# One decoder step on one core: the groups of sample value matmuls stand behind other projection units

## The reference

```python
def attn_sample(...):
    past_ckv = cache_ckv_l[page_table].reshape(db, -1, KV_LORA)
    past_kr = cache_kr_l[page_table].reshape(db, -1, ROPE_DIM)
    ...
    s_past = jnp.einsum('bthk,bsk->bhts', q_abs, past_ckv) + jnp.einsum('bthr,bsr->bhts', q_rope, past_kr)
    ...
    p = jax.nn.softmax(sc, axis=-1).astype(ckv.dtype)
    o_lat = (jnp.einsum('bhts,bsk->bthk', p[..., :n_past], past_ckv)
             + jnp.einsum('bhts,bsk->bthk', p[..., n_past:], ckv))
    ...
def combine(x, gate, att, g_att, pool, g_pool, w_out):
    mixed = jnp.concatenate([att * jax.nn.silu(g_att), pool * jax.nn.silu(g_pool)], axis=-1)
    return x + gate[:, None, :] * jnp.einsum('bte,ed->btd', mixed, w_out)
```

## Time and profile before

| | us |
|---|---|
| median of 3 runs | 1618.17 |
| lowest and highest run | 1617.62, 1657.11 |
| span of the profiled execution | 1616.8 |
| PE busy in it | 1483.7 (92%) |
| DVE busy | 780.6 (48%) |
| ACT busy | 651.9 (40%) |
| POOL busy | 493.5 (31%) |

### The profile page before, as it was taken

One profiled execution on the slowest core, in us unless ns is written; L12 is line 12 of the kernel. 1 busy time (PEld: TensorE's weight loads), 2 busy tenths in 40 slices (PEclk: granted clock), 3 DMA queues, 4 the chain that ended last, 5 costly groups with the idle time before them and its releaser, 6 DMA issues. The chain is left out here.

```text
span 1616.8 us, 24423 instructions
## 1 busy us (share of the span) xinstructions
PE 1483.7 (92%) x8584; PEld 1236.4 (76%) x8584; DVE 780.6 (48%) x1594; ACT 651.9 (40%) x1296; POOL 493.5 (31%) x423
## 2 busy tenths in 40 slices
PE   7787799999999589999999999999848999999997
PEld 1487689999998467777777787877627888888886
DVE  0587532223321677766676767664252333333333
ACT  0255322222110556565666666666631222222221
POOL 0355523232221524343443434343331111111100
PEclk9899899999999799999999999999957999999999
DMA  9243221111101200000000000000065144434310
GB/s 367 94 126 110 84 87 53 53 53 52 58 27 47 52 1 11 11 8 12 8 12 8 14 4 14 7 7 11 15 244 181 60 157 156 155 122 146 124 60 28
DMA packets 71502, 114.70 MB, mean 71 GB/s; under 512 B 33236, under 2 KB 50548, under 8 KB 69205
## 3 DMA queue, kind: packets, MB, share of 16 engines
q1 hardware_dynamic: 58782, 70.73, 13.8%
q0 software_dynamic: 3456, 27.26, 4.6%
q10 hardware_dynamic: 9168, 15.50, 2.7%
HBM read 90.95 MB, written 22.77 MB: 70 GB/s over the span
## 5 line engine op out<-in xcount | busy, mean ns | idle before, releaser
L1177 POOL TENSOR_TENSOR pt_lo<-pt,pt_hi 128x512 fp32r<-128x512 f32 (+2 forms) x160 | 171.1, 1069 | 262.3 <-ACT pt_hi L1082 261.9
L1081 ACT ACTIVATE pt<-att_ps_s 128x512 f32<-128x512 f32 (+1 forms) x320 | 170.2, 532 | 150.9 <-PE att_ps_s L1351 85.3
L1237 DVE TENSOR_REDUCE mx<-att_ps_p 128x1 f32<-128x512 f32 (+2 forms) x300 | 177.2, 606 | 91.7 <-PE att_ps_p L1321 71.4
L1082 ACT ACTIVATE pt_hi<-att_ps_s 128x512 fp32r<-128x512 f32 (+1 forms) x320 | 169.2, 529 | 0.0
L1248 DVE TENSOR_TENSOR pt_lo<-pt,pt_hi 128x512 fp32r<-128x512 f32 (+1 forms) x160 | 120.2, 751 | 93.0 <-ACT pt_hi L1082 91.2
L107 PE MATMUL mix_ps_u<-mix_h_hi,wb_hi 128*128 128x256 f32 x512 | 146.2, 285 | 0.0
L109 PE MATMUL mix_ps_u<-mix_h_hi,wb_lo 128*128 128x256 f32 x512 | 144.9, 283 | 0.0
L108 PE MATMUL mix_ps_u<-mix_h_lo,wb_hi 128*128 128x256 f32 x512 | 144.9, 283 | 0.0
L107 PE MATMUL att_ps_o<-pt_hi,v_hi 128*128 128x512 f32 (+1 forms) x320 | 126.9, 397 | 9.3 <-DVE pt_lo L1248 8.5
L107 PE MATMUL out_ps_y<-wo_hi,mixed_hi 128*128 128x512 f32 x256 | 119.4, 466 | 2.6 <-POOL mixed_lo L1938 2.6
L1349 PE MATMUL att_ps_s<-q_hi,k_hi 97*128 97x512 f32 (+1 forms) x320 | 120.3, 376 | 1.6 <-issue 1.6
(11 more groups left out here) (348 smaller groups left out, 3316.2 us busy)
## 6 DMA issues: line engine op xcount, KB each, us to landing
ada<-in_ada_w_dram SPq DMA_DIRECT2D x8, 1536.0 KB, 15.1
lat_x<-in_x_prompt_dram SPq DMA_DIRECT2D x16, 512.0 KB, 4.3
mix_x<-in_x_prompt_dram SPq DMA_DIRECT2D x16, 512.0 KB, 3.7
x_rows<-in_x_prompt_dram SPq DMA_DIRECT2D x16, 512.0 KB
out_dram<-y ACTq DMA_DIRECT2D x16, 512.0 KB, 2.7
lat_wraw<-in_w_in_dram POOLq DMA_DIRECT2D x8, 768.0 KB
gate_att_scratch<-gate_a SPq DMA_DIRECT2D x16, 256.0 KB, 2.0
pool_scratch<-mixed SPq DMA_DIRECT2D x32, 128.0 KB, 2.0
```

The lines of the kernel that those rows point to most:

```text
L1081: act.activation(pt[:, k % 2, 0:n], ps_s[:, k % 2, 0:n], ACT.Exp, scale=SCALE)
L1082: act.activation(ph[0][:, k % 4, 0:n], ps_s[:, k % 2, 0:n], ACT.Exp, scale=SCALE).then_inc(exp_done, 1)
L1177: pool.tensor_tensor(ph[1][:, k % 4, 0:n], pt[:, k % 2, 0:n], ph[0][:, k % 4, 0:n].bitcast(F32), ALU.subtract).then_inc(p_lo_ready[1], 1)
L1237: dve.tensor_reduce(mx[:, I % 2, r, c:c + 1], chunk_bank(g, n)[:, 0:width], AX.X, ALU.max).then_inc(chunk_read, 1)
```

## The change

Before, group g of the values stood behind unit 2g, an even one. Now it stands behind unit 2g + 1, an odd one. There it stands ahead of the `turn_piece` and the `score` of the same unit.

```diff
                     if exists(i - 1, DB):
-                        if u % 2 == 0 and u // 2 < QT:
+                        if u % 2 == 1 and u // 2 < QT:
                             values(i - 1, 1 - e, u // 2)
                         if u == 2 * QT:
                             new_value(i - 1, 1 - e)
```

## The result

| | median us | runs | ratio to the kernel before, 95% interval |
|---|---|---|---|
| before | 1617.89 | 4 | |
| changed | 1638.13 (1631.36 to 1646.32) | 4 | 1.0157 (1.0106 to 1.0208) |
| changed, measured again on another occasion | 1631.46 (1628.11 to 1648.76) | 6 | 1.0105 (1.0074 to 1.0136) |

The forecast was 1616.0 us with a range of 1611.5 to 1625. The changed kernel is outside it, on the side of rival 3. The ratios leave out the runs that lie more than 1.5% above the fastest of the same kernel, while the medians take in every run, so a ratio isn't the quotient of two medians.

The account below looks back on a forecast made before the run. PE's own instruction stream was taken to bound the output stage. 48 moved groups at 0.04 us (1.9) plus 0.2 in sample 7 gain 2.1 us: span 1614.7, median 1616.0 us, range 1611.5 to 1625.

Parts of the forecast that it names:

- rival 3: Samples 1 to 6: last group ahead of unit 15's transposes and scores brings more clock falls, 3.2 us each; chance 0.27.
- What bounds the stage: Output stage: only PE's own instruction stream sets the time, busy for 331.0 of 334.0 us from 1258 to 1592 us.
- The cost of a group: PE's stream, samples 1 to 6: each value group moved from an even to an odd unit gains 0.04 us.
- 0.88 given back and 0.84 taken: Per moved group: the even unit gives back 0.88 us, the odd unit with transposes takes 0.84 us more.
- the last part of the prediction: Expected profile: even units 0.47 us, odd 2.87 and 1.75, 45.6 to 45.7 between `new_value`s without a fall, waits only in `spread`.
- the 0.04: Gain per moved group: one break less (0.09 us), transposes 0.39 in place of 0.36, 0.01 more between group and transposes.
- The prediction's other estimate: From the Trainium skill page: each pair pays 0.107 us for an uncovered load against 0.09 saved, 0.8 us slower in all.
- Rival 4: Samples 1 to 6: covered load lost in each pair, or no gain; 0.5 us more, 1618.7 us; chance 0.04.
- rival 5: Scored pieces sharing a unit with values: PE held for copies or pages, 0.1 us in each of 30, 1619.1 us; chance 0.04.
- The clock: TensorE's granted clock in the output stage was taken to do as before, giving 1616 us; chance 0.50.

## Why the prediction was wrong

**What bounds the stage: right.** PE's stream bounds it, before and after; no wait was added anywhere.

**The cost of a group: right.** 0.88 given back and 0.84 taken were measured as 0.47, 2.87 and 45.6 to 45.7 us between two `new_value`s, as the last part of the prediction had them. The three parts that the prediction gives for the 0.04 add up to 0.05 (0.09 - 0.03 - 0.01); the 0.35 measured over eight groups is 0.044. The prediction's other estimate, a covered weight load that is lost and 0.8 us slower in all, isn't borne out: undisturbed samples are 0.35 us shorter, not longer. Rival 4 falls with it, and rival 5 with the unchanged waits.

**The clock: this step failed, twice.** The forecast took the clock "as before" at a chance of 0.50. Rival 3 named the place, unit 15 ahead of one unit and `new_value`, and the direction. The first miss is its chance. The reason given against it was that sample 7 has rows of the same length "at a clock of 1.00", taken from one execution. Nine of the 13 profiles have a fall in sample 7, and in three of them one low there lasts 31, 41 or 44 us. One execution without a fall said little. The same holds for the run of 1657.11 that the prediction laid aside: in the three groups of experiments the kernel before's runs above 1655 us have a mean granted clock of 0.935 to 0.937, and its runs below 1610 one of 0.964 to 0.966.

The second miss is the price. A fall was put at 3.2 us from one of 6.8 us. In the first profile of the changed kernel three of them lasted 13.7 or 20.5 us and cost 6.3 (51.9 less 45.6) or 9.1 us; in the second profile two cost 6.3 and two 3.2. Had the price been 6 to 9, rival 3's three more falls would have given 1634 to 1643, and the range would have had to reach there. That rival's highest case, 1632 for five more falls, was too low for the same reason.

**What is shown and what is not.** Shown: the loss is lost clock and not work, and it comes with the last group's move (undone 1618.65, alone 1631.72); nearly all of it goes when two units or a filled unit stand behind unit 15 (1619.49, 1620.77). In the 13 profiles all 24 falls in samples 1 to 6 begin within 3.5 us behind the start of `new_value`, and none behind the other merged rows. Not shown: why the clock falls in one sample and not in the next with the same order, and why a low lasts 7 us in one place and 20 in another. Not shown either is what in a row of small matmuls counts, its length, its data type or its changes between kinds of work, and why sample 7, which has rows as long with only one unit between them, had no fall in four of the 13 profiles.

## What to carry to other kernels

A stream of TensorE without any hole can still lose its clock where small matmuls crowd together: look at what stands between two blocks of large matmuls, not only at the sum of starts. In this kernel it helped to leave two units behind a row of 2.3 us of small matmuls, and to shorten a row of 2.5 us to 1.8; another kernel has to be measured for it. Before a forecast within a per cent, look at the granted clock of more than one execution, and price a fall by its whole length.

## What the runs showed of the hardware

- A full engine is no guard: PE was busy for 5.00 of 5.00 us in stretches where the granted clock was 0.50.
- The time of a single-core execution follows the mean granted clock: the 77 runs of the kernel before beside the experiments reach from 1607.74 us at 0.965 to 1659.18 at 0.935. Over the 54 of the first two groups the line through them has a slope of 16 us for each 0.01 of clock, and a correlation of -0.99.
- More work can be less time: matmuls that add 4.9 us to the stream took 11 to 17 us off.
- The lows of this stage last 3.4, 6.8, 10.2, 13.7, 20.5, 31, 41 and 44 us here. At half clock a sample lost about 0.45 us for each microsecond of low (6.3 in 13.7, 9.1 in 20.5).
